# Moba's keys turned by DMA instead of TensorE, with group 2's steps moved later

## The reference, cut to what matters

```python
x = x + 0.5 * swiglu(rms_norm(x, norm_ffn1), w_ffn1_in, w_ffn1_out)
h = rms_norm(x, norm_mix)
moba_qkv, fox_qkv, fox_f, pool_u, mem_q, gate_logits = split(h @ w_in)
q_a = partial_rotary(rms_norm(q_a, moba_q_gain), positions)     # 8 heads of 64
k_a = partial_rotary(rms_norm(k_a, moba_k_gain), positions)
o_a = moba_attention(q_a, k_a, v_a)       # 256 tokens are one block: causal attention
o_b = multiscale_pool(pool_u, pool_mix, pool_scale)
o_c = forgetting_attention(rms_norm(q_c, fox_q_gain), rms_norm(k_c, fox_k_gain), v_c, log_f)
o_m = memory_cross_attention(mem_q, mem, ...)                   # 4 heads of 128
y = einsum('bsnc,ncd->bsnd', [o_a, o_b, o_c, o_m], w_branch)
x = x + sum(sigmoid(gate_logits) * y, n) @ w_out
x = x + 0.5 * swiglu(rms_norm(x, norm_ffn2), w_ffn2_in, w_ffn2_out)
```

## Time and profile before

| | us |
|---|---|
| median of 3 runs | 1319.68 (1319.03 to 1320.27) |
| the profiled execution | 1319.18 |
| its span | 1317.4 |
| PE busy in the span | 1312.9 |
| DVE busy | 931.7 |
| ACT busy | 698.1 |
| POOL busy | 320.9 |

### The profile page before, as it was taken

How to read it: one execution, slowest core, us unless ns; L and a number is a source line. 1 busy time by engine, 2 the same in 40 slices (tenths; PEclk the granted TensorE clock), 3 DMA queues, 4 the chain that set the end, 5 groups by cost and what they waited for, 6 DMA issues and landing times.

```text
span 1317.4 us, 15706 instructions
## 1 busy us (share of the span) xinstructions
PE 1312.9 (100%) x6046; PEld 1084.4 (82%) x6046; DVE 931.7 (71%) x1166; ACT 698.1 (53%) x961; POOL 320.9 (24%) x306
## 2 busy tenths in 40 slices
PE   9999999999999999999999999999999999999999
PEld 8888888888888888888888888888888888888887
DVE  6666777789998675665475664787999976665653
ACT  6444465554757454444455454555546664645442
POOL 0324312034451202323003240020424421023220
PEclk9999999999999999999999999999999999999999
DMA  8877566568766647766557785555776875568671
GB/s 319 263 212 224 173 227 205 194 168 269 211 200 194 210 156 238 223 209 217 191 192 223 210 227 194 193 157 188 222 225 200 232 203 198 182 216 224 208 215 64
DMA packets 218011, 272.57 MB, mean 207 GB/s; under 512 B 106688, under 2 KB 116816, under 8 KB 217936
## 3 DMA queue, kind: packets, MB, share of 16 engines
q1 hardware_dynamic: 216752, 268.13, 66.1%
q0 software_dynamic: 896, 3.16, 0.7%
q10 hardware_dynamic: 288, 0.27, 0.1%
HBM read 245.30 MB, written 1.06 MB: 187 GB/s over the span
## 4 chain that ended last, share of the span: by engine, by line
PE 99%; DVE 0%; issue 0%; DVEq 0%
PE psum L717 24%; PE psum L968 23%; PE psum L744 21%; PE psum L727 12%; PE psum L973 11%; PE psum L926 1%; PE psum L838 1%; PE psum L864 1%; PE psum L930 1%; PE psum L710 1%; PE psum L873 1%; PE psum L843 1%; PE psum L664 0%; PE psum L884 0%; PE psum L988 0%; PE psum L911 0%
## 5 line engine op out<-in xcount | busy, mean ns | idle before, releaser
L1463 DVE TENSOR_TENSOR ring_lo<-raw,ring_hi 128x1024 fp32r<-128x1024 f32 x459 | 598.8, 1319 | 311.0 <-ACT ring_hi L1039 309.5
L1039 ACT ACTIVATE ring_hi<-raw 128x1024 fp32r<-128x1024 f32 x462 | 480.6, 1048 | 543.9 <-PE psum L727 234.5
L717 PE MATMUL psum<-ring_hi,hT 128*128 128x512 f32 x1376 | 339.9, 389 | 0.0
L717 PEld LDWEIGHTS psum<-ring_hi,hT 128*128 128x128 f32 x1376 | 258.4, 188 | 53.6
L968 PE MATMUL psum<-ring_hi,hT 128*128 128x512 f32 x960 | 240.0, 392 | 0.0
L968 PEld LDWEIGHTS psum<-ring_hi,hT 128*128 128x128 f32 x960 | 178.6, 188 | 38.5 <-issue 1.0
L727 PE MATMUL psum<-ring_lo,hT 128*128 128x512 f32 x704 | 188.7, 390 | 0.0
L1350 POOL COPY planes<-gate 128x1024 uint16<-128x1024 uint16 (+1 forms) x48 | 68.9, 1463 | 409.7 <-DVE gate L1537 409.7
L727 PEld LDWEIGHTS psum<-ring_lo,hT 128*128 128x128 f32 x704 | 131.8, 188 | 27.1
L973 PE MATMUL psum<-ring_lo,hT 128*128 128x512 f32 x480 | 128.3, 389 | 0.0
L1360 POOL COPY prodT<-planes_T 128x512 uint16<-128x512 uint16 (+1 forms) x96 | 87.0, 973 | 102.5 <-DMA planes_T<-planes 102.5
(11 more groups left out here) (199 smaller groups left out, 1220.5 us busy)
## 6 DMA issues: line engine op xcount, KB each, us to landing
raw<-in_w_ffn_in SPq DMA_DIRECT2D x78, 1024.0 KB, 5.2
raw<-in_w_in SPq DMA_DIRECT2D x64, 1024.0 KB, 5.5
raw<-in_w_ffn_out SPq DMA_DIRECT2D x44, 1024.0 KB, 5.0
raw<-in_w_branch SPq DMA_DIRECT2D x16, 1024.0 KB, 5.8
raw<-in_w_ffn_in SPq DMA_DIRECT2D x18, 512.0 KB, 4.9
raw<-in_w_mem_kv SPq DMA_DIRECT2D x8, 1024.0 KB, 5.2
raw<-in_w_out SPq DMA_DIRECT2D x8, 1024.0 KB, 6.0
forget<-negc_rows POOLq DMA_DIRECT2D x2, 1024.0 KB, 7.1
```

Of the source, the lines that this page charges most:

```text
L717: pe.matmul(outs[t][:, :], hT[part][:, kc, t * P:(t + 1) * P], w[0][:, kc - first, :], start=kc == 0 and part == 0, stop=False)
L1039: act.activation(unit_out(0, step, k), view, ACT.Copy).then_inc(hi_done.sem, 1)
L1463: dve.tensor_tensor(unit_out(1, step, k), view, unit_out(0, step, k).bitcast(F32), ALU.subtract)\
```

## The change

Moba's keys are turned by planes on POOL and the DMA queue, as job KA_ROWS of turn_rows; SP issues its transpose behind the load of kc's second half step. The eight products per layer on PE and DVE's copy of their result are gone. The products of the gains (MEM's and FOX's q gain times k gain) are computed once per layer by DVE into both_gains (2 columns), the scaling of the queries on ACT takes them, and DVE's scaling of the keys (L1690) is gone; FOX's first scores wait for the joined keys directly. ACT does one of the three joining copies per half of group 5. And tasks move:

- group 2: scores from the middle of gate(3,0)'s first half to the middle of y(3,0), two steps later, now a task of its own on DVE at the start of that step (before, between two instructions of qc's norm); exps from gate(3,0)'s second half, START, to kc's first half, MIDDLE; planes from y(3,0) to kc's second half, MIDDLE; values on PE from the middle of gate(3,1)'s second half to the end of y(3,1), on ACT and DVE to the start of vc;
- group 3: exps from START to MIDDLE of the same step; planes from gate(3,1)'s second half to vc's first; values on PE from MIDDLE to END of the same step;
- group 4: scores on PE from MIDDLE to END of the same step;
- SP issues the transposes of group 2's planes behind the load of vc's second half step instead of y(3,1).

```diff
-        ("DVE", _step_of("gate", (1, 0)), START, 0),
+        ("DVE", _step_of("va"), START, None),
         ("PE", _step_of("gate", (1, 0), 1), END, 0), ("ACT", _step_of("gate", (1, 0), 1), END, 0),
-        ("PE", _step_of("qc", None, 1), END, 1), ("DVE", _step_of("qc", None, 1), START, 1),
-        ("ACT", _step_of("y", (3, 1)), MIDDLE, 2), ("DVE", _step_of("vc", None, 1), START, 2)):
+        ("ACT", _step_of("y", (3, 1)), MIDDLE, 2)):
...
-ROWS_BEHIND = {_step_of("qm", None, 1): 0, _step_of("qc"): 1, _step_of("gate", (3, 1), 1): 2, _step_of("gate", (0, 0), 1): 3}
+ROWS_BEHIND = {_step_of("qm", None, 1): 0, _step_of("qc"): 1, _step_of("kc", None, 1): 2, _step_of("gate", (3, 1), 1): 3,
+               _step_of("gate", (0, 0), 1): 4}
...
+TASKS.setdefault(("ACT", _step_of("gate", (2, 1), 1), START), []).append(("join", 5))
-PLANES_BEHIND = {_step_of("y", (3, 1)): 2, _step_of("gate", (0, 1)): 3, _step_of("gate", (2, 0), 1): 4, _step_of("y", (2, 0)): 5}
+PLANES_BEHIND = {_step_of("vc", None, 1): 2, _step_of("gate", (0, 1)): 3, _step_of("gate", (2, 0), 1): 4, _step_of("y", (2, 0)): 5}
...
-    (2, _step_of("gate", (3, 0)), _step_of("gate", (3, 0), 1), _step_of("y", (3, 0)), _step_of("gate", (3, 1), 1)),
-    (3, _step_of("kc", None, 1), _step_of("gate", (3, 1)), _step_of("gate", (3, 1), 1), _step_of("gate", (0, 0), 1)),
+    (2, _step_of("y", (3, 0)), _step_of("kc"), _step_of("kc", None, 1), _step_of("y", (3, 1))),
+    (3, _step_of("kc", None, 1), _step_of("gate", (3, 1)), _step_of("vc"), _step_of("gate", (0, 0), 1)),
...
-    TASKS.setdefault(("PE", scores, END if g == 1 else MIDDLE), []).append(("scores", g))
-    if g != 2:
-        TASKS.setdefault(("DVE", scores, END if g == 1 else START), []).append(("scores", g))
-    _plan("exps", g, exps, act=START)
+    TASKS.setdefault(("PE", scores, END if g in (1, 4) else MIDDLE), []).append(("scores", g))
+    TASKS.setdefault(("DVE", scores, END if g == 1 else START), []).append(("scores", g))
+    _plan("exps", g, exps, act=MIDDLE if g in (2, 3) else START)
     _plan("share", g, exps, dve=START)
...
+    if g == 2:
+        TASKS.setdefault(("PE", summed, END), []).append(("values", g))
+        TASKS.setdefault(("ACT", _step_of("vc"), START), []).append(("values", g))
+        TASKS.setdefault(("DVE", _step_of("vc"), START), []).append(("values", g))
...
 # POOL, joining the planes of groups 2 to 5
-                    for b, block_of in ((0, slice(0, 2)), (1, slice(2, 6, 2)), (2, slice(3, 6, 2))):
...
+                    for b in range(2 if g == 5 else 3):
+                        last = pool.tensor_copy(*joined(g, h, b))
...
 # POOL, the queue
                 turn_rows(L, QA_ROWS, qk[:, 0], qkT_buf[:, MOBA % 2, 0])
-                pool.wait_ge(rows_merged.sem, rows_merged.at(L, QA_ROWS + 1))
-                pool.sem_inc(qT_ready[MOBA].sem, 1)
                 turned(L, 1)
...
                 pool.dma_start(forget[:, :, P:], negc_rows[None, :, :].to_broadcast([P, NH, SEQ])).then_inc(forget_loaded.sem, 16)
+                pool.wait_ge(rotated.sem, rotated.at(L, 2))
+                turn_rows(L, KA_ROWS, qk[:, 1], qkT_buf[:, MOBA % 2, 1])
                 pool.wait_ge(taken_dve.sem, taken_dve.at(L, release("qc")))
                 turn_rows(L, QC_ROWS, qk[:, 0], qkT_buf[:, FOX % 2, 0])
...
 # DVE
-                        for b in range(2):
-                            last = dve.tensor_copy(qkT_buf[:, MOBA % 2, 1, 2 * b:2 * b + 2, :],
-                                                   bank[6 + b][:, :].rearrange("p (c t) -> p c t", c=2))
-                        last = dve.tensor_scalar(columns, columns, gain(L, HEAD_AT + at), None, ALU.mult)
+                elif stage == "head_gains":
+                    dve.tensor_tensor(both_gains[:, L, :], gains[:, L, HEAD_AT:HEAD_AT + 3:2], gains[:, L, HEAD_AT + 1:HEAD_AT + 4:2], ALU.mult)\
...
-                    head_factors(L, dst, heads, (lambda: task(L, "scores", 2)) if kind == "qc" else None)
+                    head_factors(L, dst, heads, None)
```

More of the change, by code:

```diff
@@ L349, in build @@
         squares = tally("squares", 2 * len(NORMED))
-        qkT_ps = tally("qkT_ps", 2)
+        qkT_ps = tally("qkT_ps", 1)
         qT_ready = [tally(f"qT_ready{br}", 1) for br in range(3)]
[L352 to L355, removed]
+        head_gains = tally("head_gains", 1)
+        rows_planes = tally("rows_planes", 5)
+        rows_turned = tally("rows_turned", 16 * 5)
+        rows_merged = tally("rows_merged", 5)
         scores_ready = tally("scores_ready", 6)
@@ L467, in value_out, with joined @@
             return [b[:, group_width(i):2 * group_width(i)] for b in group_banks(L, which, 2 * i)]
+        def joined(g, h, b):
+            block_of = (slice(0, 2), slice(2, 6, 2), slice(3, 6, 2))[b]
+            words = pT[:, b, :].bitcast(U16).rearrange("p (j odd s h) -> p h odd j s", j=2, odd=2, h=2)
+            return words[:, h], planes_out(g)[h].rearrange("p (odd q s) -> p odd q s", odd=2, q=6)[:, :, block_of, :]
         def halves_of(words):
@@ L810, in task @@
                 elif stage == "qkT":
[L812 to L818, removed]
-                    i = 0 if arg == MEM else 1
+                    pe.wait_ge(split_lo.sem, split_lo.at(L, 2 * SPLITS.index("mixed") + 2))
+                    pe.wait_ge(taken_dve.sem, taken_dve.at(L, release("qm")))
                     for c in range(BC):
@@ L826, in task @@
                     br, buf, c0 = heads(L, arg)
-                    pe.wait_ge(qT_ready[br].sem, qT_ready[br].at(L, 1))
-                    pe.wait_ge(kT_ready[br].sem, kT_ready[br].at(L, 1))
+                    if br != MOBA:
+                        pe.wait_ge(qT_ready[br].sem, qT_ready[br].at(L, 1))
+                    pe.wait_ge(rows_merged.sem, rows_merged.at(L, {MEM: KMEM_ROWS, MOBA: KA_ROWS, FOX: KC_ROWS}[br] + 1))
                     if arg >= 2:
@@ L1194, in task @@
                         columns = qkT_buf[:, FOX % 2, 0]
-                        last = act.activation(columns, columns, ACT.Copy, scale=gain(L, HEAD_AT))
+                        last = act.activation(columns, columns, ACT.Copy, scale=both_gains[:, L, 0:1])
                     last.then_inc(qT_ready[arg].sem, 1)
@@ L1223, in task @@
                     last.then_inc(head_planes.sem, 1)
+                elif stage == "join":
+                    act.wait_ge(head_turned.sem, head_turned.at(L, 32 * (BY_PLANES.index(arg) + 1)))
+                    for h in range(2):
+                        last = act.activation(*joined(arg, h, 2), ACT.Copy)
+                    last.then_inc(act_joined.sem, 1)
                 elif stage == "pooled":
```

37 lines of the change are left out of this document (17 added, 20 removed).

## The result

The changed kernel takes 1335.28 us (median of four runs, 1334.51 to 1337.13), the kernel before 1319.60 on the same chip: ratio 1.0123, 95% interval 1.0111 to 1.0135. I had said 1322.9, range 1317.8 to 1326.3; the loss is 15.7 us where 3.2 were forecast, and lies 9 us outside the range.

What follows compares the result with a forecast made beforehand. PE's full queue was taken as the bound, with DVE nearly full between qc and y(3,1). Per layer -0.89 + 2.5 = +1.6, two layers +3.2 us: execution 1322.4, median shown 1322.9, range 1317.8 to 1326.3.

Steps and rivals of the forecast that it cites:

- What PE loses, 1.78 us: Key transposes on PE, before y(3,0): removing them gains 0.89 us per layer, 1.78 in two.
- Edits at nothing: Key scalings, group 5's joins, gains' product, later values 3 and scores 4: cost PE nothing, price 0.
- In time by 0.6 us at the median and late by 1.1 at the worst. I take 0: Scores 2 in y(3,0): joined keys at 333.9, PE asks at 334.5; wait 0, kept 0 to +1.1 us per layer.
- Rival C: Turned data late: keys at scores 2 (1.1 us per layer) or group 3's planes (2.0): 1325.1 to 1326.9; chance 0.10.
- The chain to y(3,1): Group 2's serial chain from kc to y(3,1): PE waits 2.5 us per layer, from 1.1 to 3.9.
- my 341.54: Forecast end of PE's first unit of kc, where group 2's chain starts: 342.43 less 0.89.
- for the first and nothing for the second: POOL's disturbances in the chain: group 2's joins 1.4 us, FOX's query joins 0; bounds 0 to 2.8.
- my 22.6 us: Time PE gives the chain, from kc's first unit's end to y(3,1)'s remainder part; undisturbed chain takes 23.7 us.
- What comes after: After y(3,1): group 2's joins, FOX's keys and group 3's planes; taken as 0, kept 0 to +2.0 us.
- Rival B: ACT's 1.28 us table load falls into the chain before group 2's exponentials: 1325.5; chance 0.12.
- Rival A: The chain holds and PE waits nowhere: 1317.9; with its half-way form 1317.5 to 1320.8, chance 0.24.
- What I said would prove me wrong: No PE gap at y(3,1), its remainder made by 364, or the largest gap elsewhere, above all at scores 2.

Runs made afterwards that it cites:

- experiment 11: Changed kernel with Moba's keys back on PE, group 2's exponentials and planes earlier, its joins on ACT, group 3's share behind y(3,1)'s first remainder: 1318.65 us, ratio 0.9995.
- experiment 12: Kernel before with only the small edits: products of gains, no DVE key scalings, ACT's join for group 5: 1318.94 us, ratio 0.9998.
- experiment 3: Changed kernel, but SP issues the keys' transpose behind the load of kc's first half step instead of its second: 1329.65 us, ratio 1.0082.
- experiment 10: Changed kernel with earlier keys' transpose, earlier group 2 exponentials and planes, later group 3 share; ACT makes group 2's joins, FOX's query and Moba's key planes: 1316.98 us.
- experiment 4: Changed kernel, but POOL waits for kc's norm before it joins group 2: 1335.40 us, ratio 1.0123.
- experiment 1: Changed kernel's order of steps, but Moba's keys turned by PE and copied by DVE as before: 1328.66 us, ratio 1.007.
- experiments 3 and 7: The second of these: changed kernel with experiment 3's edit plus group 2's exponentials and planes half a slot earlier on ACT: 1330.86 us, ratio 1.0087.

## Why the prediction was wrong

**What PE loses, 1.78 us: right.** The trace has eight products fewer in each layer (6030 for 6046 on the page), and experiment 11 prices the 16 at 1.67. I had read no gap of PE in either mixer; there was one of 0.26 and one of 0.22 us at y(3,0), and they would have been another half microsecond to win.

**Edits at nothing: right** (experiment 12).

**"In time by 0.6 us at the median and late by 1.1 at the worst. I take 0": this step failed.** The terms were mis-sized and one was missing. Against 14.1 us stood 17.95: the planes 3.0 (I had 3.94), SP's queue +1.5, the landing 7.9 (6.5), the joins 5.5 (3.67, itself a disturbed row: alone the four take 2.80, experiment 3). I had named the load that stands in front of the transpose and said it needs the remainders "made by about 322, before the planes are ready"; the load went at 322.93 and the planes were ready at 321.83. My worst case took the slowest landing but the ordinary joins, though the joins fell beside four remainders: in a stretch where DVE is 98% busy the disturbed copy is the ordinary case. The missing term is the clock: I priced a wait of PE at its length, and this one had 1.7 us of slow products behind it. Rival C had the place, at 1.1 of the 4.5 us (4.8 in the second layer).

**The chain to y(3,1): mechanism right, one term too small.** From the end of kc's first unit (345.52) the links came as sized: exponentials 3.51 (3.53), planes 2.86 (2.84), scores 3.78 (3.79), remainders 2.27 (2.27), and the planes ended at 355.4, where 351.3 plus the 4.0 us by which that unit ended later than my 341.54 had to put them. I took 1.4 us of disturbance "for the first and nothing for the second", and wrote that POOL's joins would fall on the norm. They did, and cost it 2.85 us, as much as my bound of 2.8 for both disturbances together. The row I read the earlier trace rows had one small instruction held for 0.47 us; I counted disturbances per job of POOL, when the price is per DVE instruction that runs beside it, and the norm's three Newton steps put nine of these in a row. PE's recorded waits at y(3,1) are 3.85 us. By my own measure, when the remainder part may start, it is more: 345.52 plus my 22.6 us makes 368.1, and it started at 372.40, 4.3 us late, against 2.5 and a bound of 3.9. So this term too came out above its range, if by little.

The held instructions start 0.67 to 0.71 us apart (363.22, 363.93, 364.61, and so on), and POOL's six joins took 4.16 us from 363.15 on, 0.69 each: one small instruction gets through per copy. This is what the rule that I cited says, that a DVE instruction with two SBUF inputs and a GpSimd instruction that reads SBUF exclude each other for the whole instruction (the Trainium skill, page "SBUF — State Buffer", section "Who interferes with whom"). I had put it beside the rows, seen 0.4 to 0.6 us per job in them, and stayed with the rows. Rule and rows did not differ in the size of one hold; I had failed to count the holds, and the rows show one for each copy that the chain meets: six here, 2.9 us. One reading of the rows was empty, too: I wrote that scores read from PSUM were not lengthened, but the scores of the earlier trace rows ran from 350.44 to 352.25, while POOL rested (348.4 to 353.3).

**"What comes after", 0 to +2.0: right at 0.** No wait for group 2's or group 3's values. **Rival B is out:** the load went with the tanh, off the chain.

```profile
332.63 1.28 ACT L1278 ACT_TABLE_LOAD   x1
```

**Rival A** (the chain holds, 1317.9) is what the version of experiment 10 reaches, at 1316.98, with the copies on ACT. It was not this change.

**What I said would prove me wrong** was a gap "at scores 2 above all"; it is one of two equal ones. Removing the first returned 5.0 of its 9 us (experiment 3), because the longer single wait at y(3,1) then cost clock as well.

## What to carry to other kernels

Where an engine is 98% busy beside a full PE, price a copy put on GpSimd by what VectorE runs next to it, instruction by instruction; a chain of small dependent VectorE instructions was the worst neighbour here (2.9 us on 4.75), and moving the copies behind it halved their cost to the chain and no more. Give such copies to an engine that did not meet VectorE: ScalarE had 16 of 52 us free and took them with no wait of PE. A transfer's place in its issuing queue is part of its latency: look at what the instruction ahead of it waits for. And a wait of PE is not priced at its length: here waits of 2.5 to 3.7 us in one piece were mostly, not always, followed by slow products that cost another 1.5 to 1.9 us, so an edit can shorten the waits and not the time (experiment 4).

## What the runs showed of the hardware

- Instructions of VectorE on 128x16 with two SBUF inputs: 0.17 us alone, 0.63 to 0.67 beside GpSimd's 16-bit copies, one per copy. A TENSOR_SCALAR with one input was held in the same way (128x16, 0.65 us at 358.86 in the kernel before, where the group's joins ran until 359.5). The copies suffer too: six joins 4.2 us beside the small instructions, 8.5 beside shares and remainders; four joins 2.80 us ahead of the remainders, 5.51 beside them.
- The same 128x1024 16-bit plane copy: 1.0 us on ScalarE, 1.0 to 2.0 on GpSimd.
- After the waits of 2.64 and 2.96 us at scores 2 PE's granted clock fell to about half (0.52 over 337 to 340), and the slow products cost 1.7 us each time; after those of 2.85 and 2.73 us at y(3,1) the products took 0.39 to 0.40 us from the second on, full speed. In experiment 1 two waits of 2.74 us at the same place of the two layers differ: the products behind the first take 0.39 us, behind the second 0.63. Waits of 2.50 us (experiment 4) were followed by slow products as well. So the length of a wait alone doesn't decide it, and what does no experiment here separated.
- A transpose of one tensor's rows landed 4.4 us after GpSimd's last plane copy where nothing stood ahead of it in SP's queue (338.70 to 343.13, FOX's queries after the change), 4.9 to 7.7 where it was issued at once with loads behind it (experiments 3 and 7, both layers), 9.4 and 10.1 with the load ahead.
